# A two-layer encoder with a mixture of experts: tile 1's first gather in two parts, counting moved into the first group, and finer steps in the last group

## The reference, cut to what matters

```python
def hier_moe(x, w_group, w_expert, w1, w3, w2):
    ...
    y = jnp.zeros_like(t)
    for e in range(N_EXPERTS):                    # 16 experts, D = 1024, D_EXPERT = 512
        h = jax.nn.silu(t @ w1[e]) * (t @ w3[e])
        y = y + combine[:, e:e + 1] * (h @ w2[e])
    return y.reshape(B, S, D)

for i in range(DEPTH):                            # DEPTH = 2
    ...
    x = x + o @ w_o[i]
    x = x + hier_moe(rmsnorm(x, ln_ffn[i]), w_group[i], w_expert[i], w1[i], w3[i], w2[i])
```

## Time and profile before

| | us |
|---|---|
| median of 3 runs | 643.09 |
| lowest, highest | 642.6, 646.12 |
| the profiled execution, its own time | 643.09 |
| span of its profile | 641.3 |
| TensorE busy in it | 625.2 (97%) |
| VectorE, ScalarE busy | 178.1, 138.9 |
| DMA, mean over the span | 359 GB/s |

### The profile page before, as it was taken

One profiled execution on the slowest core, in us unless ns is written; L12 is line 12 of the kernel. 1 busy time (PEld: TensorE's weight loads), 2 busy tenths in 40 slices (PEclk: granted clock), 3 DMA queues, 4 the chain that ended last, 5 costly groups with the idle time before them and its releaser, 6 DMA issues.

```text
span 641.3 us, 10454 instructions
## 1 busy us (share of the span) xinstructions
PE 625.2 (97%) x4401; PEld 262.2 (41%) x4401; DVE 178.1 (28%) x601; ACT 138.9 (22%) x368; POOL 53.5 (8%) x61
## 2 busy tenths in 40 slices
PE   9999999999999999998999999999999999999996
PEld 5445545524324234332244455463343243343231
DVE  1665833502102102100133757253111021021011
ACT  2136642210000000000131677231100000000011
POOL 0015420000000000000010475000000000000000
PEclk9999999999999999999999999999999999999999
DMA  8999909599999999999999996596999999999992
GB/s 309 293 270 423 375 2 391 201 411 421 420 421 420 421 421 421 421 420 421 398 283 246 395 405 210 223 361 252 423 420 422 419 422 421 421 420 420 422 403 79
DMA packets 44247, 229.94 MB, mean 359 GB/s; under 512 B 8271, under 2 KB 8561, under 8 KB 20642
## 3 DMA queue, kind: packets, MB, share of 16 engines
q1 hardware_dynamic: 42556, 224.66, 89.5%
q0 software_dynamic: 1312, 4.23, 2.0%
q10 hardware_dynamic: 326, 0.31, 0.2%
HBM read 228.10 MB, written 1.08 MB: 357 GB/s over the span
## 4 chain that ended last, share of the span: by engine, by line
PE 84%; DMA 8%; DVE 3%; ACT 2%; issue 1%; POOL 0%; SPq 0%; DVEq 0%; ACTq 0%
PE ps L1400 28%; PE ps L1412 17%; PE ps L1170 12%; DMA ring<-in_w_dram 8%; PE ps L1257 8%; PE ps L1362 4%; PE ps L1369 2%; PE ps L1239 2%; PE ps L1205 2%; PE ps L1226 2%; PE ps L1467 1%; ACT attw L557 1%; PE ps L1382 1%; PE ps L1324 1%; PE ps L1124 1%
## 5 line engine op out<-in xcount | busy, mean ns | idle before, releaser
L1400 PE MATMUL ps<-attw,work 128*32 128x512 f32 x1216 | 140.1, 593 | 0.0
L1412 PE MATMUL ps<-ring,work 128*32 128x512 f32 x960 | 105.0, 593 | 1.3 <-ACT work L628 1.3
L1400 PE MATMUL ps<-ring,work 128*32 128x512 f32 x832 | 100.6, 594 | 2.4 <-DMA ring<-in_w_dram 2.4
L1170 PE MATMUL ps<-attw,work 128*128 128x512 f32 x192 | 87.4, 598 | 0.3 <-DVE work L735 0.3
L1400 PEld LDWEIGHTS ps<-attw,work 128*32 128x32 f32 x1216 | 40.1, 110 | 89.1 <-issue 89.1
L1257 PE MATMUL ps<-attw,work 128*128 128x512 f32 x128 | 59.6, 601 | 0.7 <-issue 0.5
L1412 PEld LDWEIGHTS ps<-ring,work 128*32 128x32 f32 x960 | 30.3, 110 | 70.9 <-issue 68.6
L977 DVE TENSOR_TENSOR work<-work,ps 128x256 f32<-128x256 f32 (+1 forms) x24 | 11.5, 507 | 159.7 <-PE ps L1400 159.7
L1400 PEld LDWEIGHTS ps<-ring,work 128*32 128x32 f32 x832 | 27.8, 110 | 60.2 <-issue 56.1
L1170 PEld LDWEIGHTS ps<-attw,work 128*128 128x128 f32 x192 | 34.6, 190 | 38.2 <-issue 37.4
L431 POOL TENSOR_SCALAR attw<-attw,stat 128x256 f32<-128x256 f32 x40 | 41.0, 1029 | 51.4 <-DVE stat L853 51.2
(11 more groups left out here) (155 smaller groups left out, 470.2 us busy)
## 6 DMA issues: line engine op xcount, KB each, us to landing
ring<-in_w_dram SPq DMA_DIRECT2D x112, 1024.0 KB, 26.2
attw<-in_w_dram SPq DMA_DIRECT2D x80, 1024.0 KB, 19.3
attw<-in_w_qkv_dram SPq DMA_DIRECT2D x4, 2048.0 KB, 18.6
attw<-in_w_o_dram SPq DMA_DIRECT2D x8, 1024.0 KB, 22.5
attw<-in_w_qkv_dram SPq DMA_DIRECT2D x8, 512.0 KB, 13.0
ring<-bias_rows POOLq DMA_DIRECT2D x16, 256.0 KB, 7.1
x_sb<-in_x_dram SPq DMA_DIRECT2D x2, 512.0 KB, 6.9
out_dram<-x_sb SPq DMA_DIRECT2D x2, 512.0 KB, 4.6
```

The lines of the kernel that those rows point to most:

```text
L1170: last = pe.matmul(ps[:, g, :], xT[:, k, P * tt:P * tt + P], wqkv[part][:, k, :], start=(k == 0), stop=(k == KB - 1))
L1400: last = pe.matmul(ps[row:row + SLOTS, bank[t], :], xg[:, k, t, row:row + SLOTS], w[:, e, k % 4, :], start=(k == 0), stop=(k == KB - 1), t ...
L1412: last = pe.matmul(ps[row:row + SLOTS, bank[t], :], hT[t][:, k, row:row + SLOTS], w[:, e, k % 2, 512 * half:512 * half + 512], start=(k == ...
```

## The change

**Start of the experts.** The gather of tile 1's first half of the features is cut in two: two of its four products, then `up_first(2, 0)`, then w1 on these two blocks, then the signal, and only then the other two products. VectorE copies the two blocks with a signal of their own (`first_copied`). `count` goes into group 0 behind the two transposes of `pg`, into another bank; `see_overflow` goes behind the weighing of the places; TensorE waits for its flag ahead of w3.

**Last unit.** Unit 47 (`LAST`) is still two DMAs of 1 MB, cut by rows of w2 (4 KB for each partition and expert) instead of by expert (8 KB for each partition), the second on a semaphore of its own. TensorE uses the first rows for both output halves, waits, then the second rows for both.

**Last group.** w3 with `kh` 1 begins with blocks 4 and 5 of pair 0 as soon as unit 42 is there, then waits for unit 43; blocks 6 and 7 follow by tile. Tile 1's turned h goes to two banks, ScalarE copies it in two parts, and w2 starts after the first part; the second is waited for ahead of the other output half.

```diff
+TURNS = TT * GROUPS + 1
+LAST = UNITS * GROUPS - 1
@@ SyncE
-                for n in range(HELD + 2, UNITS * GROUPS):
+                for n in range(HELD + 2, LAST):
                     wait_used(L, n - HELD)
                     load_held(L, n)
+                wait_used(L, LAST - HELD)
+                load_half(L, LAST, 0)
+                load_half(L, LAST, 1, last_half_landed)
@@ ScalarE, moe_group
-                    for t, bank in enumerate((W[0], V[0])):
-                        act.wait_ge(m.ht_done, TT * Q + t + 1)
-                        act.copy(hT[t].rearrange("p k s -> p (k s)"), ps[:, bank, :]).then_inc(m.ht_copied, 1)
+                    turns = [(0, slice(0, FB), W[0]), (1, slice(0, FB), V[0])]
+                    if g == GROUPS - 1:
+                        turns[1:] = [(1, slice(0, 2), V[0]), (1, slice(2, FB), W[1])]
+                    for n, (t, ks, bank) in enumerate(turns):
+                        act.wait_ge(m.ht_done, TURNS * R + TT * g + n + 1)
+                        act.copy(hT[t][:, ks, :].rearrange("p k s -> p (k s)"),
+                                 ps[:, bank, 0:P * (ks.stop - ks.start)]).then_inc(m.ht_copied, 1)
@@ VectorE
+            def copy_first_blocks(L):
+
+                dve.wait_ge(first_gathered, L + 1)
+                scale_gathered(L, 1, 0, 6, slice(0, 2)).then_inc(first_copied, 1)
...
                 weigh_places(1, g).then_inc(m.pc_built, 1)
+                if m is main and g == 0:
+                    see_overflow(L)
...
-                see_overflow(L)
-                copy_gathered(L, main, GROUPS * L, 1, 0, 6)
+                copy_first_blocks(L)
+                copy_gathered(L, main, GROUPS * L, 1, 0, 6, slice(2, 4))
@@ TensorE, moe_group
                     last.then_inc(m.pc_turned, 1)
+                    if begun:
+                        count(V[1])
                     up_pair(0, 1, 1)
                     pe.wait_ge(m.pct_copied, Q + 1)
+                    if begun:
+                        pe.wait_ge(flag_ready, R + 1)
                     for p in range(2):
                         up_pair(1, 0, p)
                     for p in range(2):
                         landed(up_unit(1, 1, p))
+                        if not fetch:
+                            for k in (4, 5):
+                                up(g, 1, k, both(p), unit)
                     for t in range(TT):
-                        for k in range(4, KB):
+                        for k in range(4 if fetch else 6, KB):
...
-                            last = pe.transpose(ps[:, bank, P * k:P * k + P], h_sb[t][:, P * k:P * k + P], ident)
-                        last.then_inc(m.ht_done, 1)
+                            split = t and not fetch
+                            to = ps[:, W[1], P * k - 2 * P:P * k - P] if split and k >= 2 else ps[:, bank, P * k:P * k + P]
+                            last = pe.transpose(to, h_sb[t][:, P * k:P * k + P], ident)
+                            if k == FB - 1 or split and k == 1:
+                                last.then_inc(m.ht_done, 1)
...
+                            if final and p and kh and not fetch:
+                                for half in range(2):
+                                    down(g, p, kh, half, unit, [0])
+                                pe.wait_ge(last_half_landed, 16 * (R + 1))
+                                for half in range(2):
+                                    down(g, p, kh, half, unit, [1]).then_inc(m.w2_used, 1)
+                                continue
                             for half in range(2):
+                                if not fetch and p == kh == 0 and half:
+                                    pe.wait_ge(m.ht_copied, TURNS * R + TURNS)
@@ TensorE, start of the experts
                 pe.wait_ge(main.pg_built, GROUPS * L + 1)
-                count()
                 pe.wait_ge(x_scaled, TT * (L + 1))
-                gather(main, 1, 0, 6)
+                gather(main, 1, 0, 6, range(2))
                 up_first(2, 0)
-                pe.wait_ge(main.xg_copied[1][0], Q0 + 1)
-                pe.wait_ge(flag_ready, L + 1)
+                pe.wait_ge(first_copied, L + 1)
                 up_first(0, 1)
                 up_first(1, 1).then_inc(first_half_used, 1)
+                gather(main, 1, 0, 6, range(2, 4))
                 pe.wait_ge(main.xg_copied[0][1], Q0 + 1)
                 gather(main, 1, 1, 7)
                 up_first(3, 0)
+                pe.wait_ge(main.xg_copied[1][0], Q0 + 1)
                 up_first(2, 1)
```

More of the change, by code:

```diff
@@ L250, in encoder @@
         extra_landed = [sem(f"extra_landed{L}") for L in range(DEPTH)]
-        first_half_used = sem("first_half_used")
+        first_half_used, last_half_landed = sem("first_half_used"), sem("last_half_landed")
+        first_gathered, first_copied = sem("first_gathered"), sem("first_copied")
         def up_banks(g):
@@ L335, in load_held, with load_half @@
                     load_to(held[n % HELD], L, n, held_landed[n % HELD])
-            def load_half(L, n, half):
+            def load_half(L, n, half, landed=None):
                 part = slice(UNIT // 4 * half, UNIT // 4 * half + UNIT // 4)
                 src = unit_source(L, n).rearrange("e p k f -> p e (k f)")[:, :, part]
-                sp.dma_start(held[n % HELD].rearrange("p (e f) -> p e f", e=2)[:, :, part], src).then_inc(held_landed[n % HELD], 16)
+                sp.dma_start(held[n % HELD].rearrange("p (e f) -> p e f", e=2)[:, :, part], src).then_inc(landed or held_landed[n % HELD], 16)
             def wait_used(L, n):
@@ L409, in _ @@
                 if L + 1 < DEPTH:
-                    wait_used(L, UNITS * GROUPS - 1)
+                    wait_used(L, LAST)
                     load_held(L + 1, 0, 1, 2)
@@ L903, in see_overflow @@
                 dve.wait_ge(counts_done, L + 1)
-                step(dve.tensor_reduce(sum_g[:, 0:1], ps[:, 0, 64 + TT * E:64 + 2 * TT * E], AX, ALU.max))
+                step(dve.tensor_reduce(sum_g[:, 0:1], ps[:, up_banks(0)[1][1], 0:TT * E], AX, ALU.max))
                 dve.tensor_scalar(flag[:, L:L + 1], sum_g[:, 0:1], float(SLOTS), None, ALU.is_gt).then_inc(flag_ready, 1)
@@ L954, in build_gather, with scale_gathered, copy_gathered @@
                 build_places(1, g).then_inc(m.pg_built, 1)
-            def copy_gathered(L, m, Q, t, kh, bank):
+            def scale_gathered(L, t, kh, bank, part):
+                count = part.stop - part.start
+                ks = slice(4 * kh + part.start, 4 * kh + part.stop)
+                return dve.tensor_tensor(xg[:, ks, t, :], ps[:, bank, :].rearrange("p (k c) -> p k c", k=4)[:, part],
+                                         next_gains[:, L, ks].unsqueeze(2).broadcast_to([P, count, P]), ALU.mult)
+            def copy_gathered(L, m, Q, t, kh, bank, part=slice(0, 4)):
                 dve.wait_ge(m.gathered, 2 * TT * Q + 2 * t + kh + 1)
-                by = next_gains[:, L, 4 * kh:4 * kh + 4].unsqueeze(2).broadcast_to([P, 4, P])
-                dve.tensor_tensor(xg[:, 4 * kh:4 * kh + 4, t, :], ps[:, bank, :].rearrange("p (k c) -> p k c", k=4), by,
-                                  ALU.mult).then_inc(m.xg_copied[t][kh], 1)
+                scale_gathered(L, t, kh, bank, part).then_inc(m.xg_copied[t][kh], 1)
+            def copy_first_blocks(L):
+                dve.wait_ge(first_gathered, L + 1)
+                scale_gathered(L, 1, 0, 6, slice(0, 2)).then_inc(first_copied, 1)
             def moe_group(L, m, R, g):
@@ L1334, in rank, with count @@
                               start=True, stop=True).then_inc(pos_done, 1)
-                def count():
-                    pe.matmul(ps[:, 0, 64 + TT * EXPERTS:64 + 2 * TT * EXPERTS], ones[:, :], rt[7][:, 0:TT * EXPERTS],
+                def count(bank):
+                    pe.matmul(ps[:, bank, 0:TT * EXPERTS], ones[:, :], rt[7][:, 0:TT * EXPERTS],
                               start=True, stop=True).then_inc(counts_done, 1)
@@ L1356, in _, with gather @@
                 turn_added(L, 1, 1)
-                def gather(m, t, kh, bank):
-                    for k in range(4):
+                def gather(m, t, kh, bank, ks=range(4)):
+                    for k in ks:
                         c = (4 * kh + k) * P
                         last = pe.matmul(ps[:, bank, P * k:P * k + P], x_sb[:, t, c:c + P], pg_flat[:, t, :], start=True, stop=True)
-                    last.then_inc(m.gathered, 1)
+                    last.then_inc(m.gathered if ks[-1] == 3 else first_gathered, 1)
                 def scatter(m, Q):
@@ L1402, in up, with down @@
                     return last
-                def down(g, p, kh, half, unit):
+                def down(g, p, kh, half, unit, ks=range(2)):
                     W, V = up_banks(g)
@@ L1408, in down @@
                     w = w2_view(unit(down_unit(p, kh)))
-                    for k in range(2 * kh, 2 * kh + 2):
+                    for k in (2 * kh + k for k in ks):
```

(3 more changed lines are left out.)

4 lines of the change are left out of this document (2 added, 2 removed).

## The result

| | before | after |
|---|---|---|
| median of 5 executions, us | 643.09 | 639.25 |
| lowest, highest | 642.6, 646.12 | 638.97, 639.49 |
| the profiled execution, its span | 643.09, 641.3 | 639.49, 637.7 |
| TensorE, ScalarE busy | 625.2, 138.9 | 624.8, 139.0 |

After / before is **0.9925, 95% interval 0.9897 to 0.9953**: faster by 0.75%.

The account below looks back on a forecast made before the run. TensorE, 97% busy, and the weight stream were both taken as nearly full in the experts' stage, TensorE waiting once a layer. -2.81 - 0.84 - 0.1 + 0.06 = -3.69 us from 643.09 gave 639.4 us, own range 638.9 to 640.2.

Parts of the forecast that it names:

- The stall at w3's second half: Last group of each layer: TensorE waits for weights, costing 1.54 us in layer 1 and 1.27 in layer 0.
- The rival in which units 42 and 43 land together: At w3's second half: finer w3 hides nothing, stall shrinks only by the earlier stream; 640.7 us, chance 0.07.
- The rival in which the stream bounds a step later, at w2: Last groups: w2 waits for weights, so layer ends follow the stream's start; 641.6 us, chance 0.06.
- h in finer steps: Last group, tile 1: fewer transposes and a shorter copy ahead of w2; -0.42 us a layer, -0.84 us.
- Start of the experts: Each layer's experts' start: stream 0.76 us earlier as margin, TensorE gains 0.05 us a layer; -0.1 us in all.
- Last unit by rows: End of w2: the scatter starts as before and the last rows are not late; +0.06 us for both layers.
- w3 in finer steps: Last group: work on unit 42 covers the wait for unit 43, whole stall goes; -2.81 us for both layers.
- The stream's 0.76 us: Weight stream starting 0.76 us earlier in the experts' stage: worth nothing by itself without the stall, only margin.

Follow-up runs that it names:

- experiment 2: Only the finer w3 of the last group put on the kernel before: mean 641.08 us, ratio to before 0.9929.
- experiment 11: Changed kernel, tile 1's first two transposes of h waiting only for the first part of its multiply, second try: mean 638.23 us, ratio to before 0.9889.
- experiment 1: The kernel before run again without edit: twelve executions from 641.77 to 648.77 us, median 644.5, ratio 0.9984.
- experiments 2 to 8, 11 and 12: Single parts put on the kernel before, the changed kernel with parts undone, with earlier transposes, or unedited: means from 638.23 to 642.75 us.
- experiment 9: Kernel before with five unused products ahead of the last groups' wait for w3's second half: mean 643.91 us, ratio to before 0.998.
- experiment 10: Changed kernel with the weight stream released later, behind `up_first(2, 1)`, first issue 3.33 us later: mean 645.43 us, ratio to before 1.0009.
- experiment 6: Changed kernel with the old start of the experts (tile 1's gather whole, `count` in its old place): mean 640.04 us.
- experiment 5: The changed kernel run again without edit: mean 639.09 us, ratio to before 0.9915.

## Where the prediction held, and the step that failed

**The stall at w3's second half: the mechanism was right, its size was not (below).** In the changed kernel's profile the path is 17.67 and 17.68 us, as forecast, and no wait took its place. The rival in which units 42 and 43 land together is excluded by experiment 2. The rival in which the stream bounds a step later, at w2, occurs in no profile of the changed kernel; its grain of truth is that the margin at unit 43 is thin (experiments 2 and 11).

**h in finer steps: right.** From the first transposes of h to w2 it takes 1.92 and 1.91 us instead of 2.36 and 2.35, -0.44 us a layer against -0.42; tile 1's own part is 613.58 - 612.68 = 0.90 us, as forecast. The part was not run by itself; this stands on the trace.

**Start of the experts: right in direction, short in size.** 118.93 to 130.96 is 12.03 us instead of 12.32, a gain of 0.29 (forecast 0.27). Behind it, from the transposes of `pg` of group 0 to those of the next group, 50.35 us instead of 50.21, so `count` costs 0.14 us there, not 0.22: -0.15 us a layer against -0.05. VectorE's copy was no loss: the 24 records from 120.57 to 123.28 take 2.71 us, as forecast without a wait, though a row there names `L970`. The stream's first issue at 123.42, with the start of the stage 0.23 us later, is 0.73 us earlier by that stage's clock (forecast 0.76).

**Last unit by rows: right.** w2 of pair 1 begins 7.03 us ahead of its scatter (622.52 to 629.55), 7.01 before; forecast +0.03 us. There is no gap ahead of the scatter, in the matmuls at the end of layer 1:

```profile
622.52 7.07 PE L1434 MATMUL ps<-ring,work 128*32 128x512 f32 x64
629.55 1.99 PE L1404 MATMUL ps<-work,ropet 64*128 64x512 f32 x8
```

So the sum held between the two profiled executions: forecast -3.69 us, measured -3.60 (the four terms as measured give 3.95 us, and the profiled execution of after reached the experts 0.23 us later). **The step that failed is the size of the term "w3 in finer steps", -2.81 us.** The prediction read the two stalls, 1.27 and 1.54 us, from one execution, took them as the kernel's, and allowed "some 0.3 between executions". Of 75 executions of before, 20 took at most the 643.09 us of the profiled one; their mean is 644.73 and they reach to 649.58. Seventeen of after have a mean of 638.96 and reach from 637.94 to 639.6. The gain over executions is 5.8 us, 0.9%: 3.6 us between the profiled ones, 1.64 because the profiled execution of before was a good one, 0.53 because that of after was the slowest of its five. The first ratio, on five executions each, lies between. The other three terms measured 0.88, 0.30 and -0.04 us of gain, so an estimate of 4.6 us is left for the term that had 2.81; by itself, in experiment 2, it measured 3.9 us with a standard error of 0.6.

Two things were left out of that size. First, **the stall differs from execution to execution**: in the profiles at hand the stream took from 169.35 to 171.7 us for the same bytes, and the stall in the kernel before was 1.2 to 4.4 us. Second, **a long stall can cost clock on top**: 1.7 of the 4.4 us in experiment 1. In 21 of the 70 executions of before beside the experiments the mean clock is 0.996 or below, and none of these is under 644.5 us; in the 61 executions of experiments 2 to 8, 11 and 12 none has such a clock. The mean clock is a rough sign, though. It also falls when TensorE has done its last work, where that costs nothing, as in the changed kernel's profile, whose mean is 0.998:

```profile
635.00:636.00 1.00, 0.00 (x0) 0.00 (x0) 0.00 (x0) 0.00 (x0) 0.00 (x0) 0.50 0.31 113
```

And 0.997 can hide a costly fall (experiment 9). The nine profiles of these 61 executions show no fall ahead of the program's end. The fine w3 and the earlier stream together take TensorE out of most of that spread, not all of it (experiment 11).

A second step of the prediction falls with it: "The stream's 0.76 us is worth nothing by itself once the stall is gone; it is margin." Against one execution that is so; with a stream that varies, margin is time whenever it runs out. Experiments 2 and 11 show it running out in a profile, and experiment 10 lost 6.8 us by a stream 3.33 us later. What the 0.76 us themselves are worth in the changed kernel is not resolved: experiment 6 lost 0.95 us, 0.3 of it TensorE's own work, with an interval from 0.2 to 1.7.

The Trainium skill, TensorE: Matmul & The Clock Gate, section Part 1: The HAM clock gate, tells of the same two levels, 1.2 GHz after idling and 2.4 GHz after activity, and puts the penalty of the ramp from one to the other at under 1% of a typical kernel span. The rows agree: 1.7 us is 0.3% of this span. Yet here it is more than the whole stall of a layer in the profile that the prediction was made from.

**Left open**: why the stream's length varies by some 2 us (windows of 17 us in two profiles of before show 418 to 422 GB/s in both from 141 us on; 1% of the stream is 1.7 us, so they single out no place); why 1.9 us of idling was followed by half clock in experiment 9 and not in experiment 10; what the last unit's rows are worth; and why the first transposes of the experts start anywhere between 130.45 us (experiment 5) and 133.00 (experiment 2), part of the spread that is left.

## What to carry to other kernels

A stall on a transfer stream that runs at its full rate is one draw in one profile: look at the spread of the execution times, and at the granted clock behind the stall, before you size it, since the worst draws can also pay for clock. Work on the piece that came first, ahead of the wait for the next, hides a stall. A wait that is missing from one profile can come back in another execution, so margin ahead of such a stream counts, though here its worth was shown only where it ran out. When a step is cut finer, look at each wait of the new step: here the transposes still waited for a part of the multiply that they did not need.

## What the runs showed of the hardware

- One stream of 1 MB loads at some 420 GB/s took 169.35 to 171.7 us from its first issue to the landing of the same unit, in different layers and executions.
- After idle stretches of 2.5 and 2.83 us (experiments 1 and 10), and after 1.90 us in experiment 9, TensorE's granted clock was 0.50 for some 3 us; after 0.76 to 1.89 us at the same wait in other layers and profiles it stayed at 1.00. Each fall cost 1.5 to 1.7 us over the 48 to 64 records behind it.
- The granted clock also fell to 0.50 in the last microseconds of a program, behind TensorE's last work. So mean clocks of 0.997 to 0.999 say little, and one of 0.997 held a fall that cost 1.6 us (experiment 9).
- ScalarE's copies out of PSUM took 376 ns for 256 columns and 585 ns for 512, in the rows of the changed kernel grouped by line and form:

```profile
L637 ACT COPY work<-ps 128x512 f32<-128x512 f32 x14 | 8.2, 585 | 110.1 <-PE ps L1498 110.1
L637 ACT COPY work<-ps 128x256 f32<-128x256 f32 x4 | 1.3, 376 | 0.4 <-PE ps L1498 0.4
```
